# Attention of three mixers: values stationary instead of weights, weights divided by their sums before they are turned, outputs left upright

## What is computed

```python
def dilated_attention(q, k, v):
    ...
    branches = [dilated_branch(q, k, v, w, d, slopes) for (w, d) in ATT_PATTERNS]
    m_all = functools.reduce(jnp.maximum, [br[1] for br in branches])
    for n_g, m_g, d_g in branches:
        e = jnp.exp(m_g - m_all)
        num = num + n_g * e[..., None]
        den = den + d_g * e
    return (num / den[..., None]).reshape(b, s, ATT_WIDTH)
```

```python
p_c = masked_softmax(s_c, ...); o_c = jnp.einsum('bgrqn,bngd->bqgrd', p_c, vc)
p_s = masked_softmax(s_s, dist_s >= 0); o_s = jnp.einsum('bqgrm,bqgmd->bqgrd', p_s, vs)
p_w = masked_softmax(s_w, ...); o_w = jnp.einsum('bqgrk,bkgd->bqgrd', p_w, vw)
o = gs[..., 0:1] * o_c + gs[..., 1:2] * o_s + gs[..., 2:3] * o_w
...
o_nsa = rms_norm(o_nsa, nsa_out_g)
return jnp.concatenate([o_nsa, o_ret], axis=-1) @ w_out
```

## Time and profile before

| | us |
|---|---|
| median of 3 runs | 3170.62 |
| lowest and highest | 3170.51, 3170.66 |
| span of the profiled execution | 3170.4 |
| the executions' own time beside that span | 3170.5 to 3170.7, so some 0.2 lie around the span |
| PE busy in the span | 3135.0 |
| DVE, ACT, POOL busy | 1328.9, 1184.5, 1339.5 |
| PE waiting for another engine, all waits | 26 |

### The profile page before, as it was taken

The page is one execution under the profiler, slowest core; times in us unless marked ns, Lnnn a source line. Parts: engine busy times, 40 slices in busy tenths (PEclk is TensorE's granted clock), DMA queues, the critical chain, the costliest instruction groups (busy, mean ns, idle before and its releaser), DMA issues.

```text
span 3170.4 us, 42468 instructions
## 1 busy us (share of the span) xinstructions
PE 3135.0 (99%) x16760; PEld 2651.8 (84%) x16760; DVE 1328.9 (42%) x2479; ACT 1184.5 (37%) x2036; POOL 1339.5 (42%) x865
## 2 busy tenths in 40 slices
PE   8999999999999999999999999999999999999998
PEld 6877888888888987888888889888897888798887
DVE  7675533115330345746453304432055665363311
ACT  5454323223222344554432223322244554442221
POOL 4442444453444452452344444444533354334443
PEclk9999999999999999999999999999999999999999
DMA  4221233332333241231223332333432132223332
GB/s 161 80 67 47 87 107 93 100 113 67 93 101 102 77 142 59 68 102 59 81 80 102 94 97 87 100 93 100 122 93 87 48 100 81 73 69 98 102 97 67
DMA packets 80933, 285.14 MB, mean 90 GB/s; under 512 B 8928, under 2 KB 11360, under 8 KB 80480
## 3 DMA queue, kind: packets, MB, share of 16 engines
q1 hardware_dynamic: 79728, 278.59, 29.3%
q10 hardware_dynamic: 1008, 3.84, 0.3%
HBM read 280.30 MB, written 2.10 MB: 89 GB/s over the span
## 4 chain that ended last, share of the span: by engine, by line
PE 94%; DVE 2%; POOL 2%; ACT 1%; issue 1%; DMA 1%; ACTq 0%; POOLq 0%; DVEq 0%
PE bank L269 23%; PE bank L271 23%; PE bank L270 23%; PE bank L277 4%; PE bank L278 4%; PE bank L279 4%; PE bank L1497 3%; PE bank L1467 2%; POOL wlo L263 2%; PE bank L1481 1%; PE bank L3405 1%; PE bank L3431 1%; PE bank L603 1%; ACT whi L249 0%; DMA raw<-wstream 0%
## 5 line engine op out<-in xcount | busy, mean ns | idle before, releaser
L263 POOL TENSOR_TENSOR wlo<-raw,whi 128x1024 fp32r<-128x1024 f32 (+3 forms) x775 | 1218.2, 1587 | 1451.8 <-ACT whi L249 1418.1
L269 PE MATMUL bank<-hhi,whi 128*128 128x512 f32 x2080 | 820.4, 394 | 12.5 <-DVE wlo L263 10.8
L270 PE MATMUL bank<-hlo,whi 128*128 128x512 f32 x2110 | 822.4, 390 | 0.0
L271 PE MATMUL bank<-hhi,wlo 128*128 128x512 f32 x2080 | 811.1, 390 | 0.0
L249 ACT ACTIVATE whi<-raw 128x1024 fp32r<-128x1024 f32 (+2 forms) x502 | 501.2, 1031 | 361.6 <-PE bank L271 291.8
L269 PEld LDWEIGHTS bank<-hhi,whi 128*128 128x128 f32 x2080 | 391.4, 188 | 95.7 <-issue 16.6
L270 PEld LDWEIGHTS bank<-hlo,whi 128*128 128x128 f32 x2110 | 397.1, 188 | 81.6 <-issue 1.4
L271 PEld LDWEIGHTS bank<-hhi,wlo 128*128 128x128 f32 x2080 | 391.1, 188 | 82.8
L269 PE MATMUL bank<-ff_ahi,whi 128*128 128x512 f32 x660 | 256.7, 389 | 0.0
L271 PE MATMUL bank<-ff_ahi,wlo 128*128 128x512 f32 x660 | 256.7, 389 | 0.0
L270 PE MATMUL bank<-ff_alo,whi 128*128 128x512 f32 x630 | 245.1, 389 | 0.0
(11 more groups left out here) (427 smaller groups left out, 5271.4 us busy)
## 6 DMA issues: line engine op xcount, KB each, us to landing
raw<-wstream SPq DMA_DIRECT2D x508, 512.0 KB, 3.5
raw<-wstream SPq DMA_DIRECT2D x20, 256.0 KB, 2.6
xa_v<-memT ACTq DMA_DIRECT2D x2, 1024.0 KB, 4.8
outT<-x SPq DMA_DIRECT2D x4, 512.0 KB, 2.8
raw<-wstream SPq DMA_DIRECT2D x4, 420.0 KB, 4.3
x<-xT ACTq DMA_DIRECT2D x2, 512.0 KB, 7.6
x<-xT SPq DMA_DIRECT2D x2, 512.0 KB, 7.7
consts<-consts SPq DMA_DIRECT2D x1, 1004.0 KB, 8.1
```

The source lines that it names most:

```text
L263: last = g.tensor_tensor(h.lo[:, o:o + step], h.raw[:, o:o + step], h.hi[:, o:o + step].bitcast(F32), ALU.subtract)
L269: t.matmul(out, l[0], r[0], start=start, stop=False)
L270: t.matmul(out, l[0], r[1], start=False, stop=False)
L271: return t.matmul(out, l[1], r[0], start=False, stop=stop)
```

## The change

What it does:

- `pe_out` works on a pair of units at once. The values are stationary (128 keys by 64 features) and the turned weights move (128 keys by 128 queries). Unit e = 0 writes partitions 0 to 63 of the bank and unit e = 1 partitions 64 to 127, in turns. An output has features in partitions: it is upright for the output projection. All heads and branches of a query tile (or, in `MixerOne`, all query tiles of a head pair) add up in one bank.
- Since queries are no longer in partitions there, sums and gates can't be applied to the output. DVE now inverts the sums for every pair of units (`dve_weights`), multiplies by the gates (`gate`) and scales the weights in place before they are turned (`dve_scale`): over 512, 384, 256 or 128 columns of `att_s`.
- `pe_turn` and ACT's exponential and copy stand behind the first two filler steps of a step (`BEFORE_TURN = 2`), and `pe_turn` waits for the scaling.
- `SplitOutputs` (`MixerOne`): ACT and DVE make high and low parts out of the bank. `NormOutputs` (`MixerTwo`): ACT copies a query tile's bank to `up` and squares it, DVE adds the squares of the four tiles, PE adds over the partitions with a one-column matmul, DVE makes the mean, POOL one root for all four query tiles, PE lays the roots along a row (`pe_rows`, within the first half of the output projection), and DVE scales `up` by that row and makes the low parts.
- The transposes of `o_tok`, the tensors `o_tok` and `scaled`, and the steps `finish`, `act_norm`, `dve_norm`, `pool_norm` are gone. On the host the rows of the output weights and the gain are permuted so that tile j holds heads j and j + 4.

Counted over the program: 400 matmuls of 64 moving columns become 400 of 128 with a stationary of 64; 16 of 256 columns (the compressed branch) become 64 of 128 with a stationary of 64; 48 transposes go; 8 transposes and 8 matmuls of one column come.

The core of the diff:

```diff
-        for o, n, place, value in self.pieces[i]:
-            at, nb = place * width, n // P
-            for kb in range(nb):
-                last = t.matmul(k.bank[b][:, at:at + width], p[:, o + kb * P:o + (kb + 1) * P], value(kb), start=kb == 0,
-                                stop=kb == nb - 1, skip_group_check=True)
+        t.wait_ge(*self.kept[2 * r + 1])
...
+        for m, both in enumerate(zip(self.pieces[2 * r], self.pieces[2 * r + 1])):
+            for kb in range(both[0][1] // P):
+                for e, (o, n, at, value) in enumerate(both):
+                    last = t.matmul(k.bank[b][DH * e:DH * e + DH, at:at + P], value(kb), self.probT[e][:, o + kb * P:o + (kb + 1) * P],
+                                    start=self.opens(r) and m == 0 and kb == 0, stop=True, skip_group_check=True)
...
     def pe(self, others, per_unit):
+        for now, turn, out, _, fillers in self.steps(per_unit):
+            if now is not None:
+                self.pe_scores(2 * now)
+            if out is not None:
+                self.pe_out(out)
+            for n in range(fillers):
+                if n == self.BEFORE_TURN and turn is not None:
+                    for e in range(2):
+                        self.pe_turn(2 * turn + e)
                 next(others, None)
+            if out is not None and self.closes(out):
+                self.left.pe(self.tiles[out])
...
+    def dve_weights(self, r):
...
+        v.wait_ge(*self.exped[2 * r + 1])
+        v.tensor_scalar(inverse, total, 1e-30, None, ALU.max).then_inc(self.floored.sem)
+        v.wait_ge(*self.floored[r])
+        v.reciprocal(inverse, inverse).then_inc(self.inverted.sem)
+        if self.gate is not None:
+            v.wait_ge(*self.inverted[r])
+            self.gate(r, inverse).then_inc(self.weights.sem)
+
+    def dve_scale(self, i):
...
+        elif self.even(i):
...
+            last = v.tensor_tensor(parts, parts, each, ALU.mult)
+        else:
+            for m, (o, n, _, _) in enumerate(pieces):
+                last = v.tensor_scalar(s[:, o:o + n], s[:, o:o + n], weights[:, m:m + 1], None, ALU.mult)
+        last.then_inc(self.scaled.sem)
...
+    def act(self, tb, done):
+        a.wait_ge(*done)
+        a.activation(self.by_tile(self.up)[:, :, tb * P:(tb + 1) * P], self.by_tile(k.bank[self.b][:, :]), ACT.Copy).then_inc(self.kept.sem)
+        if tb > 0:
+            a.wait_ge(*self.added[tb - 1])
+        a.activation(self.squares(tb), k.bank[self.b][:, :], ACT.Square).then_inc(self.sq.sem)
+    def dve(self, tb):
+        v.tensor_reduce(self.total, self.squares(tb).rearrange("p (j q) -> p q j", j=4), AX_X, ALU.add).then_inc(self.added.sem)
+    def pe(self, tb):
+        t.wait_ge(*self.added[tb])
+        t.wait_ge(*self.kept[tb])
+        t.matmul(k.bank[self.b][:, 0:1], self.total, k.c("ones"), start=True, stop=True, skip_group_check=True).then_inc(self.sums.sem)
```

More of the change, by code:

```diff
@@ L1519, in act_exp @@
             return
-        if self.sums_before[g] is not None:
-            a.wait_ge(*self.weights[self.sums_before[g]])
-        for m, (o, n, place, _) in enumerate(self.pieces[i]):
+        if self.sums_before[r] is not None:
+            a.wait_ge(*self.weights[self.sums_before[r]])
+        total = self.of_unit(i, self.sums(r)[0])
+        for m, (o, n, _, _) in enumerate(self.pieces[i]):
             part = s[:, o:o + n]
-            last = a.activation(part, part, ACT.Exp, bias=self.neg_max(i)[:, m:m + 1], accum_out=self.sums(g)[0][:, place:place + 1])
+            last = a.activation(part, part, ACT.Exp, bias=self.neg_max(i)[:, m:m + 1], accum_out=total[:, m:m + 1])
         last.then_inc(self.exped.sem)
@@ L1599, in dve, with even @@
-    def dve(self, others, per_unit, finish):
-        k, v = self.k, self.k.nc.vector
-        for now, turn, out, fillers in self.pairs(per_unit):
-            for i in now:
-                self.dve_scores(i)
-            for i in turn:
-                self.dve_weights(i)
-            for i in out:
-                if self.last[i]:
-                    g = self.group[i]
-                    width = (self.place[i] + 1) * self.units[i].get("heads", 1) * DH
-                    v.wait_ge(*self.pv[i])
-                    v.wait_ge(*self.weights[g])
-                    finish(g, k.bank[self.bank(g)][:, 0:width], self.sums(g)[1])
+    def even(self, i):
+        pieces = self.pieces[i]
+        return len(pieces) > 1 and all(piece[1] == pieces[0][1] for piece in pieces)
@@ new lines, in dve @@
+    def dve(self, others, per_unit):
+        for now, turn, out, before, fillers in self.steps(per_unit):
+            if before is not None and self.closes(before):
+                self.left.dve_after(self.tiles[before])
+            if turn is not None:
+                self.dve_weights(turn)
+                for e in range(2):
+                    self.dve_scale(2 * turn + e)
+            if now is not None:
+                for e in range(2):
+                    self.dve_scores(2 * now + e)
+            if out is not None and self.closes(out):
+                self.left.dve(self.tiles[out])
@@ L1617, in pool @@
     def pool(self, others, per_unit):
-        for _, _, _, fillers in self.pairs(per_unit):
+        for _, _, _, _, fillers in self.steps(per_unit):
             for _ in range(fillers):
@@ L1788, in shifted @@
         yield itertools.islice(steps, 16)
-def with_step(steps, after, other):
-    for n, _ in enumerate(steps):
-        yield
-        if n + 1 == after:
-            next(other)
-            yield
 class MixerOne:
@@ L2653, in __init__ @@
         self.at_weights = put.at[0]
-        units, self.tiles = [], []
+        units, self.rows = [], []
         for qb in range(TB):
```

426 lines of the change are left out of this document (217 added, 209 removed).

## The result

The changed kernel takes 3175.75 us (median of 20 executions, 3170.02 to 3181.47) against 3170.86 us for the kernel before (20 executions, 3170.31 to 3172.05). The ratio is 1.0013 with a 95% interval of 1.0007 to 1.0019: a loss of 0.13%, clear of the noise, but inside the 0.2% that the prediction had called the least that tells. Forecast were 3142 us, in a range of 3127 to 3167. The executions of the changed kernel also spread over 11 us, those of before over 2.

What follows compares the result with a forecast made beforehand. The prediction took PE's issued work to bound the kernel; terms for products, transposes, switches, ends and waits summed to −28.4 us against 3170.6, giving 3142 us, range 3127 to 3167.

Steps and rivals of the forecast that it cites:

- What bounds the kernel: Whole kernel: PE is busy 3135 of 3170.4 us, so time is the sum of what PE issues, plus waits.
- Values products: Attention's values matmuls on PE: 800 records become 400 concurrent pairs in two column halves, 92 to 48.4 us, −43.6.
- Both rivals about the array: Values products: stationary loads not hidden, 3167 us, chance 0.11; or column halves not running at once, 3193 us, chance 0.12.
- compressed branch: Compressed branch's values matmuls on PE: 32 records become 64 pairs, 7.0 to 7.2 us, +0.2.
- openings: Start of each run of paired values records: 0.1 us each; bound without this cost −5.6 us.
- Switches: Turning behind two fillers: PE's kind of work changes more often, 0.15 us a step over 64 steps, +9.6.
- Ends of mixer two: Last pair-steps without fillers: PE waits for scales, copies and sum of squares, 3.5 against 0.6 us, twice, +5.8.
- DVE and ACT: Added inverses, gate products and scaling passes in each attention step: they fit narrowly, residual PE waits +3, bounds 0 and 15.
- DVE becomes the bound: Densest steps of mixer two: POOL holds up DVE's scales, 21 us in two layers, 3165 us, chance 0.07.
- its own sign: PE's waits for DVE's scales summing to 15 us or more around 1300 to 1350 us mean DVE is the bound.
- The clock: PE's granted clock, 1.00 throughout: no idle stretch was expected to lower it; below 1.00 the sum would be wrong.

Runs made afterwards that it cites:

- f11: Changed kernel with both units' values products in the same column half, still in turns (computes something else): 3208.59 us.
- e2: Changed kernel without the two scaling passes, turning waits only for the exponential (no division or gates): 3141.96 us.
- e1: Changed kernel with DVE's inverse, gating and scaling moved into the pair's own step, behind four filler steps: 3164.01 us.
- e3: Changed kernel without the two scaling passes, turning waits for the inverse and gate product, their place in DVE's queue kept: 3154.84 us.
- e4: Changed kernel with useless fp32 matmuls ahead of the wait for scaling at three turnings in each layer of mixer two: 3167.47 us.
- f9: Changed kernel with inverse and gates in the pair's own step, ACT scaling mixer two's one-piece units, and the last sum of squares 12 matmuls later: 3148.09 us.
- e5: Changed kernel with values products not in turns, all of unit 0 ahead of unit 1: 3183.0 us.

## Why the prediction was wrong

It was wrong in the time by 34 us and in the sign. Its steps, in its own order:

- **What bounds the kernel**: right, and it stayed PE.
- **Values products, −43.6**: nearly. Blocks take 0.81 and 1.02 us for 0.74 and 0.96 by its prices, 56 blocks × 0.065 = 3.6 us too much credit. Both rivals about the array are ruled out by the records' starts and by f11. The compressed branch had a slip: eight openings of 0.1 on 6.85 are 7.65, not 7.2. Its blocks take 1.02 for 0.97, +0.4 for +0.2, which does not matter.
- **Switches, +9.6**: nearly. One step was priced at 5.4 us and takes 5.50, the extra switch included; attention one as a whole gains 9.2 us. In e2, where nothing stands in the way, a step with 16 records is 0.70 us shorter than before with its products 0.81 shorter, one with 12 records 0.46 with 0.58: 0.11 to 0.12 a step, some 7 us in all.
- **Ends of mixer two, +5.8**: right. 4.5 for the sum, 2.6 for copies, less the 0.5 and 0.7 us of before: 5.9.
- **DVE and ACT, +3 between 0 and 15**: this is the step that failed. Measured are 20.2 us of waits, outside its bounds. It added up one loop (5.0 us against a step of 5.4 or 7.7) and the busy time of a window (39.2 of 50 us) and found that both fit. Neither says when the scales run. DVE takes its queue in order, and the scales of a step had been put behind all of the filler's DVE work of the step before, which comes in bursts of up to 6 us and in one case behind a 5.25 us wait for POOL, while PE reaches the turning after 1.4 us of cover. The question it asked elsewhere, what is queued ahead, was not asked of DVE. Its price of a pass, 0.474, is that of a pass with POOL idle; half of those over 512 columns take 0.91 to 0.96. The rival "DVE becomes the bound" had the right engine, 21 us and a chance of 0.07, and its own sign, waits for the scales of 15 us or more, came true if not all in the stretch it named; its mechanism, POOL holding the passes up, is there in the trace. But e1 and e3 show that it is not all: with the order alone changed the waits for scales fell to 4.5 us, and without any pass 8.5 us of waiting in the queue stayed. How much of the 20.2 POOL makes was not isolated.
- **The clock, not in the sum**: the sentence that nothing gives PE an idle stretch by which the clock would fall was false as soon as the waits were there. 13.6 us, two thirds of the stalls once more. It also contradicts the forecast's own end of mixer two, with its 2.1 us of idle PE.

The sum with these put in: −28.4 + 3.6 + 17.2 (20.2 for 3) + 13.6 = +6.0 us, against +5.5 between the spans. That it closes so well is partly luck: the switches were some 2 us too dear, and a wait costs about 0.17 more than the list says (the turning at 1285.11 comes 1.97 after the next dense matmul could have started, listed as 1.80), 2.5 us for the fifteen. What the forecast priced without DVE is borne out by e2, and exceeded by 4.5 us. e2 has the matmuls, switches and ends of the change but not its passes. It is 28.9 us faster than before, where by the forecast less its 3 us, with 3.6 for the products and 3.4 for the clock, it would be 24.4. So the gain is real and was given back, 20 us to DVE's lateness and 14 to the clock.

The range has a slip as well: the bounds named for switches, waits and openings add up to 3127 to 3163, not 3128 to 3158; the measured time is outside of both.

## What to carry to other kernels

When a change puts an operation of another engine on the way between two steps of the bound engine, a busy share with room in it and a loop that fits do not show that it comes in time: follow that engine's queue in the trace and see what work, and whose waits, stand ahead of it at the densest step. Price that engine's operations by the rows in which its neighbour works, if it will: here a pass over 512 columns costs 0.48 us with POOL idle and 0.94 beside it. Price a stall of PE like these (1.8 to 4 us) with the half-speed stretch behind it, here 1.7 us on top in three cases of four, and nothing or 3.4 in the others. And if an operation is late by its place, moving it ahead only helps if what it overtakes has slack; a neighbour engine with a free queue (ACT here) gave what no reordering did.

## What the runs showed that was not expected

- Idle PE mostly costs twice. Behind 35 of 42 stalls of 1.8 to 4 us PE ran at 0.50 for 3.4 us or twice that, and filling six stalls with useless matmuls won 8 us (e4). f9 still has stalls of up to 1.7 us, and no 5 us window of its stages is below 1.00.
- Column halves overlap fully only when the matmuls take turns: 16 records take 1.02 us in turns, 1.51 with four matmuls of one half ahead of four of the other, and 1.89 in one half (changed kernel, e5, f11). In all three each record has a new stationary, and no load shows.
- DVE operations took about twice as long beside POOL's work: passes over 512 columns 0.91 to 0.96 us, where they take 0.48 to 0.49 with POOL idle; a floor of eight columns took up to 2.24 for 0.17, and the inverse of two columns (L1609) took 0.17 either way. How much of the 20 us of stalls this makes stays open: no run took POOL's work away.
